# Reordered work at the ends of the feed-forwards of an fp32 decoder step: two panels' low parts on VectorE, piece buffers exchanged, new lists for the last chunk and the entries

## The reference, cut

```python
def sq_relu_mlp(xn, w_up, w_down):
    h = jax.nn.relu(xn @ w_up)
    return (h * h) @ w_down
# layer 0: h += hgrn2_mixer(rmsnorm(h)) ; h += sq_relu_mlp(rmsnorm(h))
# layer 1: k, v = rmsnorm(h, g_kv) @ w_kv ; q = rmsnorm(h) @ w_q_b
#          h += stick_breaking(q, k, v) @ w_out_b ; h += sq_relu_mlp(rmsnorm(h))
return rmsnorm(h, g_final), states, k, v
```

## Time and profile before

| | |
|---|---|
| median of 3 runs | 1528.14 us (1527.84 to 1528.20) |
| profiled execution | 1528.13 us, span 1526.4 us |
| TensorE, matmuls | 1487.9 us, 97% of the span, 13024 |
| VectorE | 1181.8 us, 77%, 1997 |
| ScalarE | 823.4 us, 54%, 1296 |
| GpSimd | 338.3 us, 22%, 322 |
| mean granted TensorE clock | 0.993 |
| chain that ended last | TensorE 92%, VectorE 4% |

### The profile page before, as it was taken

The page is one execution under the profiler, slowest core; times in us unless marked ns, Lnnn a source line. Parts: engine busy times, 40 slices in busy tenths (PEclk is TensorE's granted clock), DMA queues, the critical chain, the costliest instruction groups (busy, mean ns, idle before and its releaser), DMA issues.

```text
span 1526.4 us, 33777 instructions
## 1 busy us (share of the span) xinstructions
PE 1487.9 (97%) x13024; PEld 1412.7 (93%) x13024; DVE 1181.8 (77%) x1997; ACT 823.4 (54%) x1296; POOL 338.3 (22%) x322
## 2 busy tenths in 40 slices
PE   8999999999999999998899999999999999999988
PEld 8999999989999999998898888888799999999988
DVE  7866666658998989888735888888789989898743
ACT  6544444436654636455433777777656546364533
POOL 3000000003223232322242121112232322323141
PEclk9999999999999999999999999999999999999999
DMA  6233333224776777775325565543257677787611
GB/s 188 57 86 86 85 86 86 86 86 107 151 175 151 175 165 159 178 159 136 103 81 177 190 191 187 167 153 122 88 105 170 149 166 171 160 179 154 158 56 63
DMA packets 237717, 205.83 MB, mean 135 GB/s; under 512 B 8269, under 2 KB 224405, under 8 KB 237589
## 3 DMA queue, kind: packets, MB, share of 16 engines
q1 hardware_dynamic: 151346, 147.34, 31.0%
q0 software_dynamic: 68160, 47.20, 20.2%
q10 hardware_dynamic: 18082, 9.48, 2.3%
HBM read 192.19 MB, written 11.80 MB: 134 GB/s over the span
## 4 chain that ended last, share of the span: by engine, by line
PE 92%; DVE 4%; issue 1%; ACT 1%; DMA 1%; DVEq 0%; SPq 0%; ACTq 0%
PE acc L2783 23%; PE acc L3106 18%; PE pL L3106 12%; PE pM L3106 9%; PE acc L3206 6%; PE pO L3106 3%; PE pM L3264 3%; PE acc L3044 2%; PE pL L2904 1%; PE pO L3278 1%; PE pL L3247 1%; PE acc L3321 1%; PE acc L3338 1%; PE pO L3310 1%; PE pM L2973 1%
## 5 line engine op out<-in xcount | busy, mean ns | idle before, releaser
L656 POOL TENSOR_TENSOR wlo<-wraw,whi 128x512 fp32r<-128x512 f32 x48 | 69.0, 1467 | 463.0 <-ACT whi L770 463.0
L2783 PE MATMUL acc<-xa_hi,whi 128*128 128x288 f32 x544 | 126.0, 313 | 3.4 <-issue 3.4
L839 ACT ACTIVATE hi<-wraw 128x1024 fp32r<-128x1024 f32 x60 | 63.7, 1061 | 106.5 <-PE acc L3106 106.2
L856 ACT ACTIVATE hi<-wraw 128x1024 fp32r<-128x1024 f32 x60 | 63.7, 1061 | 103.5 <-DVE wraw L1960 103.0
L3106 PE MATMUL acc<-X_hi,hi 128*128 128x288 f32 x384 | 113.3, 295 | 4.4 <-DVE lo L1981 4.4
L2783 PE MATMUL acc<-xa_hi,wlo 128*128 128x288 f32 x544 | 117.3, 297 | 0.0
L2783 PE MATMUL acc<-xa_lo,whi 128*128 128x288 f32 x544 | 117.2, 297 | 0.0
L3106 PE MATMUL acc<-X_lo,hi 128*128 128x288 f32 x384 | 113.4, 295 | 0.0
L3106 PE MATMUL acc<-X_hi,lo 128*128 128x288 f32 x384 | 113.3, 295 | 0.0
L1975 DVE TENSOR_TENSOR lo<-wraw,hi 128x1024 fp32r<-128x1024 f32 x60 | 73.3, 1222 | 46.0 <-ACT hi L839 46.0
L3106 PE MATMUL acc<-H_lo,hi 128*128 128x288 f32 x336 | 99.2, 295 | 0.0
(11 more groups left out here) (547 smaller groups left out, 5145.8 us busy)
## 6 DMA issues: line engine op xcount, KB each, us to landing
wraw<-in_w_up_dram SPq DMA_DIRECT2D x64, 512.0 KB, 5.9
wraw<-in_w_down_dram SPq DMA_DIRECT2D x64, 512.0 KB, 4.9
Kp<-in_cache_k_dram SPq DMA_DIRECT2D x32, 512.0 KB, 4.3
Vp<-in_cache_v_dram SPq DMA_DIRECT2D x32, 512.0 KB, 5.5
wraw<-in_w_in_a_dram SPq DMA_DIRECT2D x30, 512.0 KB, 5.6
S_even<-in_w_up_dram POOLq DMA_DIRECT2D x32, 256.0 KB, 5.8
wraw<-in_w_up_dram POOLq DMA_DIRECT2D x32, 256.0 KB, 4.8
S_odd<-in_w_up_dram POOLq DMA_DIRECT2D x32, 256.0 KB, 5.9
```

The lines of the kernel that those rows point to most:

```text
L656: ins = pool.tensor_tensor(wlo[s][:, k:k + 2, :], wraw[s][:, k:k + 2, :], whi[s][:, k:k + 2, :].bitcast(F32), ALU.subtract)
L839: act.activation(blocks4(hi02), by_rows(G % 2)[:, 0], ACT.Copy).then_inc(piece_hi, 1)
L856: act.activation(blocks4(hi31), by_depth(G % 2)[:, 0], ACT.Copy).then_inc(piece_hi, 1)
L2783: last = pe.matmul(acc[a][:, hf, 0:HALF], w[s][:, k, a * P:(a + 1) * P], x[k][:, hf * HALF:(hf + 1) * HALF], start=(k == 0 and n == 0), st ...
```

## The change

- Buffers: pieces 0 to 3 all lie in slot 0. `S_even` moves behind X's high parts, `S_odd` into slot 1 beside pieces 4, 5 and 6.
- Waits that go with it: the sums' high part of the first quad needs two units less; `S_odd`'s first filling needs two more; GpSimd fills the first quad's row part before its column.
- `enter_mlp`: the sums' high and low part and the corner's high part of the first quad move up in the lists of ScalarE and VectorE; block 6's add goes ahead of X's last low part but one.
- Quads 26 and 27 get lists of their own (`late_up`), quad 28's (`last_first_down`) takes over the first add, one low part and the sums' and corner's low parts that `last_pairs` had put into quad 27. `last_down` takes `h_part_3` earlier.
- The low parts of panel U_Q//2 and of panel U_MLP1//2 go from GpSimd to VectorE, ahead of `h_part_5` and of `add_first`. The high parts wait for the sums' low part of the last quad only. Quad 59 gets a list of its own (`last_up`).

```diff
 hi02, lo02 = (two(n, a, F32R, a + PIECE) for n, a in (("hi02", hi0_at), ("lo02", lo0_at)))
-hi31, lo31 = (two(n, a + 2 * PIECE, F32R, b + PIECE) for n, a, b in (("hi31", hi0_at, hi1_at), ("lo31", lo0_at, lo1_at)))
+hi31, lo31 = (two(n, a + 2 * PIECE, F32R, a + 3 * PIECE) for n, a in (("hi31", hi0_at), ("lo31", lo0_at)))
 hi4, lo4 = (sb_at(n, [P, 1, PIECE // 4], F32R, a)[0] for n, a in (("hi4", hi1_at), ("lo4", lo1_at)))
 hi56, lo56 = (two(n, a + 2 * PIECE, F32R, a + 3 * PIECE) for n, a in (("hi56", hi1_at), ("lo56", lo1_at)))
-S_at = [[hi0_at + 3 * PIECE, lo0_at + 3 * PIECE], [xa_at + PAIR_BYTES, xa_at + PAIR_BYTES + PIECE]]
+S_at = [[xa_at + PAIR_BYTES, xa_at + PAIR_BYTES + PIECE], [hi1_at + PIECE, lo1_at + PIECE]]
 S_even, S_odd = two("S_even", S_at[0][0], F32, S_at[0][1]), two("S_odd", S_at[1][0], F32, S_at[1][1])
...
-def last_pairs(G):
-
-    return place(G)[1] == FCH - 1 and place(G)[2] > 1
-
 def pair_two_before(G):
-    if G % N_Q0 < 2 or not (is_up(G - 1) and is_up(G - 2)) or plain(*place(G - 2)[0:2]) or last_pairs(G):
+    if G % N_Q0 < 2 or not (is_up(G - 1) and is_up(G - 2)) or plain(*place(G - 2)[0:2]):
         return None
...
     def weight_sums(G):
-        w = weights(G)
-        if G % N_Q0 < 2:
-            pool.wait_ge(unit_done, (U_MLP0, U_MLP1)[G // N_Q0] - 2)
-        else:
-            pool.wait_ge(piece_lo, 4 * (G - 2) + 4)
+        n, w = G // N_Q0, weights(G)
         column = blocks4(outer_sums(G))[:, 1]
-        pool.dma_start(column, w[:, 0, 0]).then_inc(column_sum[G % 2], 16)
+        def column_in():
+            if G % N_Q0 < 2:
+                pool.wait_ge(unit_done, (U_MLP0, U_MLP1)[n] - (2, 0)[G % N_Q0])
+            else:
+                pool.wait_ge(piece_lo, 4 * (G - 2) + 4)
+            pool.dma_start(column, w[:, 0, 0]).then_inc(column_sum[G % 2], 16)
+        if G % N_Q0:
+            column_in()
         pool.wait_ge(raw_in[G % 2], 32 * (G // 2 + 1))
...
         pool.dma_start(by_rows(G % 2)[:, 1, 0], w[:, 1, 1], accum_op=ALU.add).then_inc(row_sum, 16)
+        if G % N_Q0 == 0:
+            column_in()
         pool.wait_ge(column_sum[G % 2], 32 * (G // 2) + 16)
...
         weight_sums(G)
-    split_low(U_Q // 2, U_OB // 2)
+    pool.wait_ge(lo_done, U_Q // 2 + 1)
+    split_low_panel(1, U_Q // 2 + 1)
+    split_low(U_Q // 2 + 2, U_OB // 2)
     def split_low_unit(a):
...
         weight_sums(G)
-    split_low(U_MLP1 // 2, U_END // 2)
+    pool.wait_ge(lo_done, U_MLP1 // 2 + 1)
+    split_low_panel(1, U_MLP1 // 2 + 1)
+    split_low(U_MLP1 // 2 + 2, U_END // 2)
...
         if G in (0, N_Q0):
-            act.wait_ge(unit_done, (U_MLP0, U_MLP1)[G // N_Q0])
+            act.wait_ge(unit_done, (U_MLP0, U_MLP1)[G // N_Q0] - 2)
         else:
...
         x_high(e, 2, 1)
+        sums_high(G0)
         block(6)
...
         block_square(6, call)
+        corner_high(G0)
         block(7)
-        sums_high(G0)
         operand_high(X_hi[:, 3, 1:3, :], X_f[:, 3, 1:3, :], (xs_done, NB * n + 8))
-        corner_high(G0)
         last_high(e, X_hi, X_f, slice(4, 6))
...
             blocks_high(*behind)
-            if last_pairs(G):
-                differences_high(*behind)
         elif behind is not None:
...
             norm_rstd(call)
+    def late_up(G):
+        behind = place(G - 1)
+        last_sums_high(G)
+        square_pair(G - 1)
+        copy_out(G, "A", 0, 1)
+        copy_out(G, "C", 3, 2)
+        raw_high(G + 1)
+        copy_out(G, "A", 1, 4)
+        blocks_high(*behind)
+        if place(G)[2] == 2:
+            sums_high(G + 1)
+            corner_high(G + 1)
+            differences_high(*behind)
+            copy_out(G, "D", 2, 5)
+        else:
+            differences_high(*behind)
+            copy_out(G, "D", 2, 5)
+            sums_high(G + 1)
+            corner_high(G + 1)
+    def last_up(G):
+        last_sums_high(G)
+        copy_out(G, "A", 0, 1)
+        copy_out(G, "C", 3, 2)
+        square_pair(G - 1)
+        plain_high(*place(G - 1))
+        copy_out(G, "A", 1, 4)
+        act.wait_ge(piece_lo, 4 * G + 2)
+        wsplit(0, U_MLP1 // 2, U_MLP1 // 4 + 1)
+        copy_out(G, "D", 2, 5)
     def first_down(G):
...
         square_half(G - 1, 0)
+        square_half(G - 1, 1)
+        last_sums_high(G)
         operand_high(H_hi[:, 3, 0:1, :], H_f[:, 3, 0:1, :], (squared, square_count(n, c, 3) + 1))
-        last_sums_high(G)
-        square_half(G - 1, 1)
         operand_high(H_hi[:, 3, 1:3, :], H_f[:, 3, 1:3, :], (squared, square_count(n, c, 3) + 2))
...
     up_quad(0, n_norm["mlp0"])
-    steady_quads(1, N_Q0 - 4)
+    steady_quads(1, N_Q0 - 6)
+    for G in range(N_Q0 - 6, N_Q0 - 4):
+        late_up(G)
     def first_query_panel():
         act.wait_ge(product_done, N_PC * (N_Q0 - 1) + 4)
-        act.wait_ge(piece_lo, 4 * N_Q0)
+        act.wait_ge(piece_lo, 4 * (N_Q0 - 1) + 2)
         wsplit(0, U_Q // 2, U_Q // 4 + 1)
...
     up_quad(N_Q0, n_norm["mlp1"])
-    steady_quads(N_Q0 + 1, N_Q0 + N_Q1)
-    act.wait_ge(product_done, N_PC * (N_Q0 + N_Q1 - 1) + 4)
-    act.wait_ge(piece_lo, 4 * (N_Q0 + N_Q1))
-    wsplit(0, U_MLP1 // 2, U_MLP1 // 4 + 1)
+    steady_quads(N_Q0 + 1, N_Q0 + N_Q1 - 1)
+    last_up(N_Q0 + N_Q1 - 1)
     for b in range(2):
...
         if G in (0, 1, N_Q0, N_Q0 + 1):
-            dve.wait_ge(unit_done, (U_MLP0, U_MLP1)[G // N_Q0] - 2)
+            dve.wait_ge(unit_done, (U_MLP0, U_MLP1)[G // N_Q0] - (2, 0)[G % N_Q0])
         else:
...
     def last_low(e, k, lo, hi, full):
         v = LAST_PARTS[k]
-        dve.wait_ge(t_made, 12 * e + (12, 12, 11, 12, 12)[k])
+        dve.wait_ge(t_made, 12 * e + (10, 12, 11, 12, 12)[k])
         operand_low(lo[:, 3, v, :], full[:, 3, v, :], hi[:, 3, v, :], op_base(e) + 7 + k)
     def h_add(Ub, m):
...
         raw_low(G0)
-        x_low(e, 2, 1)
         sum_three(G0)
         h_add(Ub, 6)
+        x_low(e, 2, 1)
+        sums_low(G0)
         sum_all(G0)
...
         t_4(e, 3, X_f, X_f[:, 3])
-        sums_low(G0)
         corner_low(G0)
...
             sums_low(G + 1)
-        if split and last_pairs(G):
-            blocks_low(*behind)
-            differences_low(*behind)
-        if i == 3 and c == FCH - 1:
-            add_first(G)
-            if more:
-                corner_low(G + 1)
-            relu_half(G, 0)
         if behind is not None and not split:
...
+    def late_up(G):
+        behind = place(G - 1)
+        add_first(G - 1)
+        add_second(G - 1)
+        corner_low(G)
+        relu_pair(G - 1)
+        if place(G)[2] == 2:
+            last_sums_low(G)
+            difference_13(*behind)
+            difference_2(*behind)
+            difference_4(*behind)
+            raw_low(G + 1)
+            sum_three(G + 1)
+            blocks_low(*behind)
+            sum_all(G + 1)
+            sums_low(G + 1)
+        else:
+            differences_low(*place(G - 2))
+            difference_13(*behind)
+            last_sums_low(G)
+            difference_2(*behind)
+            raw_low(G + 1)
+            difference_4(*behind)
+            sum_three(G + 1)
+            blocks_low(*behind)
+            sum_all(G + 1)
+    def last_up(G):
+        add_first(G - 1)
+        add_second(G - 1)
+        corner_low(G)
+        relu_pair(G - 1)
+        last_sums_low(G)
+        hidden_low(4)
+        hidden_low(5)
+        panel_low(0, U_MLP1 // 2)
+        add_first(G)
+        relu_half(G, 0)
+        add_second(G)
+        relu_half(G, 1)
+        hidden_low(6)
+        hidden_low(7)
     def h_add_part(G, b, t, which, k, op=ALU.add):
...
         e, raw = made(n, c), H_f[:, 3]
+        add_first(G - 1)
+        differences_low(*place(G - 2))
         add_second(G - 1)
+        relu_half(G - 1, 0)
         relu_half(G - 1, 1)
+        sums_low(G)
         t_13(e, 3, H_f, raw, (squared, square_count(n, c, 3) + 2))
+        corner_low(G)
         t_2(e, 3, H_f, raw)
         t_4(e, 3, H_f, raw)
-        for k in range(3):
-            last_low(e, k, H_lo, H_hi, H_f)
+        last_low(e, 0, H_lo, H_hi, H_f)
+        last_low(e, 1, H_lo, H_hi, H_f)
+        last_low(e, 2, H_lo, H_hi, H_f)
         h_part_1(G)
...
         last_low(e, 4, H_lo, H_hi, H_f)
+        h_part_2(G)
         last_sums_low(G)
-        h_part_2(G)
         raw_low(G + 1)
+        h_part_3(G)
         sum_three(G + 1)
         sum_all(G + 1)
-        h_part_3(G)
+        h_part_4(G)
         sums_low(G + 1)
-        h_part_4(G)
         h_part_5(G)
...
             sum_three(G + 1)
+            h_part_3(G)
             sum_all(G + 1)
-        query_low(m0)
-        h_part_3(G)
-        if more:
+            query_low(m0)
             sums_low(G + 1)
-        h_part_4(G)
-        query_low(m0 + 1)
+            h_part_4(G)
+            query_low(m0 + 1)
+        else:
+            query_low(m0)
+            query_low(m0 + 1)
+            h_part_3(G)
+            h_part_4(G)
+            panel_low(0, U_Q // 2)
         h_part_5(G)
...
     dve.wait_ge(n_rs, 2 * n_norm["mlp0"] + 2)
```

(11 more changed lines are left out.)

## The result

The changed kernel takes 1504.51 us, median of 6 runs (1503.12 to 1505.27); the kernel before on the same chip takes 1527.99 (1526.29 to 1530.14, 6 runs). Ratio 0.985, 95% interval [0.984, 0.986]: 23.5 us less, forecast 24.1. The profiled execution took 1504.54, span 1502.8, mean granted clock 0.999.

The account below looks back on a forecast made before the run. TensorE, busy 1487.9 of 1526.4 us, was taken as the bound, so only its idle and slow time could be won. The seven terms sum to 24.2 us, which off 1528.13 leaves 1503.9 (forecast 1504, range 1501 to 1508).

Parts of the forecast that it names:

- (1): Both feed-forward entries: sums' low part made earlier, corner's low part next late with 0.6 idle; gain 3.7 us in all.
- (2): Quads 26 and 27: ScalarE squares a pair before copying the first block out, TensorE's bank is late; 0.2 us lost.
- (3): Quad 28: H's low parts come earlier, 1.55 idle for the sums' low part; 13.7 us against 19.15, gain 5.4.
- (4): Quads 29 and 30: earlier third quarter-add frees last product's bank; 24.26 to 22.45 us, gain 1.8; 0.65 idle in quad 31.
- (5): Quad 31 and first w_q panel: low part in one VectorE instruction; 12.2 us instead of 14.69, gain 2.5.
- (6): First panel of the last w_down: low part on VectorE; idle about 1.0 instead of 7.34, gain 6.4 us.
- (7): Behind both late panels: all low-clock stretches gone, gain 2.5 and 2.1 us, as idle 1.08 and 2.20 brought no fall.
- fourth rival: Second quad's sums land late, their fetch starting 5.8 us later: 3.9 idle in each feed-forward, 1512 us; chance 0.03.
- third rival: Last four quads: short idle times hold TensorE at the low clock, 36 us lost, 1540; chance 0.04 with anything similar.
- first rival: Quads 28 to 31 and both panels: path stays VectorE's, idle returns in pieces, 1509 to 1510 us; chance 0.14.

Follow-up runs that it names:

- the second profile: The changed kernel itself, unedited, profiled once more on another chip: 1504.81 us (4 runs), ratio 0.985 to the kernel before.

## Why the prediction was right

It was right in the total (1504.0 against 1504.5) and in each term to 0.5 us. That the total is right to half a microsecond is in part luck: the stages give back 23.0 of the 24.2, and a first feed-forward that began 0.6 earlier made up half of the rest.

```
term                                     forecast  measured (stage before less stage after)
(1) entries                               3.7       1.50 + 1.73 = 3.2 (3.5 by the second profile)
(2) quads 26 and 27                      -0.2      -0.33
(3) quad 28                               5.4       5.30
(4) quads 29 and 30                       1.8       24.26 - 22.78 = 1.48
(5) quad 31 and the w_q panel             2.5       2.29
(6) last panel                            6.4       6.33
(7) clock behind the panels               2.5, 2.1  383.84 - 381.28 = 2.56, 65.93 - 63.83 = 2.10
sum                                       24.2      23.0, and 0.6 ahead of the first feed-forward
```

The last 0.6 (378.81 to 378.22) is no work of the change: that time varies by 3 from run to run.

(1) The first profile has 0.23 more in the first entry than the second; no wait shows it, two matmuls near its start follow 0.27 and 0.21 behind the one before (379.55 and 379.76) instead of 0.133. The next late step at the entry is the corner's low part, as named: it starts 3.70 behind the first product (381.92 less 378.22; forecast 382.27 less 378.81, 3.46), and 0.48 is idle (0.6). With the old lists on the new buffers the old lengths and the old idle time come back. So the buffers alone don't make this gain; that they are needed for it, as the prediction has it, was not tried. The fetch of the second quad was rightly costed at 0, and the delayed fetch shows why that was less safe than it looked. The prediction's fourth rival put the wait behind high and low part of the sums; the bank of quad 1's first product is wanted sooner, so a sum taken 3.2 later costs a wait of 3.4 and not one of 0.9. The case did not arise, but the reckoning of that rival named the wrong victim.

(3) Followed instruction by instruction, VectorE's new list was right to 0.3: the timeline of the changed kernel has the low part of the sums at 696.06 in a quad that starts at 693.23, the differences right behind it.

```profile
694.72 1.42 DVE L2186 SCALAR_TENSOR_TENSOR H_f<-H_f,rstd 128x576 f32<-128x576 f32 x2
696.06 1.21 DVE L2019 TENSOR_TENSOR lo<-wraw,hi 128x1024 fp32r<-128x1024 f32 x1
697.19 0.75 DVE L2034 TENSOR_TENSOR H_f<-H_f 128x576 f32<-128x576 f32 x1
```

The forecast had 1.55 idle for it, 1.27 came; that the old lists give 19.03 on the new buffers shows that the buffers alone gain nothing.

(4) Here the term was a little large (1.8 for 1.48), and the net value of the one edit behind it is only 0.65, since 0.84 of it is handed on to quad 31. The prediction had that as 0.65 idle in the next quad, and 0.60 was measured.

(5), (6) High part, low part, add, one behind the other. At the w_q panel the timeline of the changed kernel has:

```profile
737.25 1.92 ACT L777 ACTIVATE whi<-wraw 128x2048 fp32r<-128x2048 f32 x1 [2.12 <-PE pL L3191]
...
739.23 2.28 DVE L1667 TENSOR_TENSOR wlo<-wraw,whi 128x2048 fp32r<-128x2048 f32 x1
741.43 0.75 DVE L2328 TENSOR_TENSOR hT<-hT,acc 128x576 f32<-128x576 f32 x1
```

That is 4.93 from 737.25 to 742.18 where the forecast had 5.0. The doubled low part shows that this chain is the path. That at the last panel only half of the gain comes from the change of engine stands nowhere in the prediction; it reckoned the new chain from its start, which holds both halves, and so the total was right all the same.

(7) All low stretches went, as taken. The third rival (the clock held low by the many short waits) did not come: waits of 0.1 to 1.3 in quads 26 to 31, clock 1.00 throughout. The Trainium skill's "TensorE: Matmul & The Clock Gate", section "A second HAM failure mode: psum-queue depth-cycling", says that frequent very short idle times can set the clock swinging; with waits as rare as these the trace shows no such swing. But that 1.08 and 2.20 had passed without a fall was a weaker reason than it read: with quad 28's sums first, one wait of 1.99 brought the clock down, and the quad grew by 1.56 where its idle time grew by 0.72. The term held by a margin that the rows of before did not show. Its 2.1 for the last panel should have been 2.0 by its own working (19 times 0.107); 2.10 was measured.

The first rival (VectorE the bound, 1509 to 1510) is not what happened, but it is where the next gain is lost: in quad 28 VectorE is busy 13.67 of 13.85, and in quad 31 with the wait 12.31 of 12.39.
